# Last output projection tile, its norm and residual, and the first feed-forward tiles run by halves of the tokens

## What is computed

```python
    merged = jnp.sum(gates * projected, axis=2)
    x = x + rmsnorm(merged @ w_out[l], norm_mix_post[l])

    h = rmsnorm(x, norm_ffn_pre[l])
    f = (jax.nn.silu(h @ ffn_w_gate[l]) * (h @ ffn_w_up[l])) @ ffn_w_down[l]
    x = x + rmsnorm(f, norm_ffn_post[l])
```

## Time and profile before

| | |
|---|---|
| device time, median of 3 runs | 1585.75 us (1579.65, 1585.75, 1585.9) |
| span of the profiled execution | 1581.3 us |
| its own time | not given apart from its span |
| PE busy | 1508.4 us (95%), 7976 matmuls |
| DVE busy | 883.0 us (56%) |
| ACT busy | 596.3 us (38%) |
| mean DMA rate | 96 GB/s |

### The profile page before, as it was taken

One profiled execution on the slowest core, in us unless ns is written; L12 is line 12 of the kernel. 1 busy time (PEld: TensorE's weight loads), 2 busy tenths in 40 slices (PEclk: granted clock), 3 DMA queues, 4 the chain that ended last, 5 costly groups with the idle time before them and its releaser, 6 DMA issues.

```text
span 1581.3 us, 19613 instructions
## 1 busy us (share of the span) xinstructions
PE 1508.4 (95%) x7976; PEld 1205.2 (76%) x7976; DVE 883.0 (56%) x1405; ACT 596.3 (38%) x880; POOL 20.7 (1%) x36
## 2 busy tenths in 40 slices
PE   4799998999999999999999999999998999999997
PEld 2575786667787787777788887888886888888886
DVE  6889797785736763343525444643347544444234
ACT  3334415565325554232426433342333322222220
POOL 0010010000000000000000000000000000000000
PEclk8899999999999999999999999999999999999998
DMA  8433154104422111221223211232341323222221
GB/s 329 168 94 94 55 124 147 54 14 174 160 80 80 54 54 61 73 77 56 94 101 107 75 59 57 77 107 80 107 154 59 107 80 107 98 89 100 100 94 53
DMA packets 24472, 152.39 MB, mean 96 GB/s; under 512 B 3472, under 2 KB 6080, under 8 KB 8112
## 3 DMA queue, kind: packets, MB, share of 16 engines
q1 hardware_dynamic: 21872, 137.43, 24.3%
q0 software_dynamic: 2512, 13.72, 3.1%
HBM read 144.55 MB, written 7.88 MB: 96 GB/s over the span
## 4 chain that ended last, share of the span: by engine, by line
PE 86%; DVE 9%; ACT 2%; issue 1%; DMA 1%; SPq 0%; DVEq 0%; ACTq 0%
PE bank L552 85%; DVE score L2097 1%; PE bank L959 1%; DMA xr<-xT 1%; ACT w_hi L1208 1%; DVE score L2078 1%; DVE w_lo L1834 1%; DVE small L2077 1%; PE bank L891 0%; DVE sv L1791 0%; DVE rstd L1865 0%; DVE w_lo L1843 0%; DVE tval L2041 0%; DVE y_lo L1860 0%; DVE rstd L1906 0%
## 5 line engine op out<-in xcount | busy, mean ns | idle before, releaser
L552 PE MATMUL bank<-h_hi,w_hi 128*128 128x512 f32 (+1 forms) x1104 | 442.2, 401 | 13.5 <-DVE h_lo L2606 7.8
L552 PE MATMUL bank<-h_hi,w_lo 128*128 128x512 f32 (+1 forms) x1120 | 438.2, 391 | 0.0
L552 PE MATMUL bank<-h_lo,w_hi 128*128 128x512 f32 (+1 forms) x1104 | 432.0, 391 | 0.0
L1834 DVE TENSOR_TENSOR w_lo<-w_raw,w_hi 128x2048 fp32r<-128x2048 f32 (+2 forms) x106 | 239.2, 2257 | 245.1 <-ACT w_hi L1208 243.6
L1208 ACT CAST w_hi<-w_raw 128x2048 fp32r<-128x2048 f32 (+2 forms) x109 | 204.6, 1877 | 164.5 <-PE bank L552 161.6
L552 PEld LDWEIGHTS bank<-h_hi,w_hi 128*128 128x128 f32 (+1 forms) x1104 | 208.1, 188 | 73.5 <-issue 23.0
L552 PEld LDWEIGHTS bank<-h_hi,w_lo 128*128 128x128 f32 (+1 forms) x1120 | 210.9, 188 | 45.7 <-issue 0.4
L552 PEld LDWEIGHTS bank<-h_lo,w_hi 128*128 128x128 f32 (+1 forms) x1104 | 208.3, 189 | 42.9 <-issue 2.1
L552 PE MATMUL bank<-y_hi,w_hi 128*128 128x512 f32 x272 | 112.8, 415 | 4.6 <-DVE y_lo L1860 4.6
L552 PE MATMUL bank<-y_hi,w_lo 128*128 128x512 f32 x272 | 107.1, 394 | 0.0
L552 PE MATMUL bank<-y_lo,w_hi 128*128 128x512 f32 x272 | 106.9, 393 | 0.0
(11 more groups left out here) (374 smaller groups left out, 1871.2 us busy)
## 6 DMA issues: line engine op xcount, KB each, us to landing
w_raw<-wstream SPq DMA_DIRECT2D x120, 1024.0 KB, 4.8
xr<-xT SPq DMA_DIRECT2D x2, 2048.0 KB, 10.2
w_raw<-wstream SPq DMA_DIRECT2D x4, 768.0 KB, 4.2
bias_rows<-bias_table POOLq DMA_DIRECT2D x1, 2560.0 KB, 12.5
bias<-bias_rows POOLq DMA_DIRECT2D x1, 2048.0 KB, 12.4
x_saved<-xr POOLq DMA_DIRECT2D x1, 2048.0 KB, 9.6
xr<-x_saved POOLq DMA_DIRECT2D x1, 2048.0 KB, 8.1
outT<-down SPq DMA_DIRECT2D x16, 128.0 KB, 1.8
```

Of the source, the lines that this page charges most:

```text
L552: return pe.matmul(out, lhsT, rhs, start=start, stop=stop)
L1834: dve.tensor_tensor(w_low_of(s)[:, 0:kt, :], w_raw[:, i % RAW_SLOTS, 0:kt, :], hi_of(s)[:, 0:kt, :].bitcast(f32), ALU.subtract).then_inc(w ...
```

## The change

The fourth group of `out2` runs token half by token half: both feature halves for tokens 0 to 255 into two banks (semaphore `mid_done`), then for tokens 256 to 511 into two others. The post norm (statistic, root, reciprocal), the residual, `h_hi` and `h_lo` run for each half of the tokens. The statistic of half 0 is issued inside the matmuls of half 1, that of half 1 behind the first k step of `ffn_up`. PE runs `ffn_up[0]` and `ffn_up[1]` for token half 0 with four half groups at once, then for token half 1 with three, then the fourth. ACT copies the two banks of half 0 into `mo` before the next groups write there. The square for norm2 is still made for 512 tokens, in the second half. Slots of `w_hi` change parity behind `ffn_up[1]`, so that `ffn_up[2]` takes the slot of `out2[3]` and `ffn_up[3]` that of `ffn_up[0]`. DVE splits the weights of `ffn_up[2]` ahead of the seven additions for norm2 instead of behind them. `half_stats`, `half_root` and `half_rstd` replace the code of the last group too; there ACT now waits for both banks of a half before it squares the first.

```diff
-             ("y0", 8), ("y1", 8), ("merged", 8), ("norm2", 8), ("f", FT)]
+             ("y0", 8), ("y1", 8), ("merged", 8), ("norm2", 16), ("f", FT)]
...
-        sizes = {"norm0": 8, "q": 4, "k": 4, "norm1": 8, "norm2": 8, "post1": 8, "post2": 8}
+        sizes = {"norm0": 8, "q": 4, "k": 4, "norm1": 8, "norm2": 8, "post1": 10, "post2": 8}
...
-            ROOT[name] = i
+            ROOT[name] = i + (i > STATS.index("post1"))
...
-        LATE_BANKS = [3, 5, 6, LATE % GEMM_BANKS, 7, (LATE + 1) % GEMM_BANKS, (LATE + 2) % GEMM_BANKS]
+        MID_BANKS = [[(LATE + 1) % GEMM_BANKS, (LATE + 2) % GEMM_BANKS], [LATE % GEMM_BANKS, 7]]
+        LATE_BANKS = [3, 5, 6] + MID_BANKS[0] + MID_BANKS[1]
...
-            return w_wide[:, :, :] if s in WIDE else w_hi[:, s % 2]
+            return w_wide[:, :, :] if s in WIDE else w_hi[:, (s + (s > WIDE[0])) % 2]
+        def held_before(s):
+            return s - 3 if s in (WIDE[0] + 1, WIDE[0] + 2) else s - 2
...
-            for w, gr in enumerate(G["out2"]):
-                gemm(gr, "fm", h_hi, h_lo, need=AT["merged"],
-                     between=(lambda: presummed("post1")) if w == 3 else None)
-            last_stats("post1")
-            wide = [(gr, half, hi_of(gr.s), w_low_of(gr.s)) for gr, half in
-                    ((G["ffn_up"][0], 0), (G["ffn_up"][0], 1), (G["ffn_up"][1], 0))]
+            for gr in G["out2"][:3]:
+                gemm(gr, "fm", h_hi, h_lo, need=AT["merged"])
+            def half_stats(name, t):
+                c, s0 = end_cols(t), SQ0[name] + 6 + 2 * t
+                out = stat_bank(name)[:, c]
+                pe.wait_ge(root_ready, ROOT[name] + t)
+                pe.wait_ge(presum_ready, PRESUM.index(name) + 1)
+                mm(out, ones[:, :], rstd[:, c], True, False)
+                for half in range(2):
+                    pe.wait_ge(sq_ready, s0 + half + 1)
+                    mm(out, ones[:, :], sqb[:, half, c], False, half == 1).then_inc(sq_used, 1)
+            gr = G["out2"][3]
+            wh, wl = hi_of(gr.s), w_low_of(gr.s)
+            pe.wait_ge(w_low, gr.s + 1)
+            for half in range(2):
+                pe.wait_ge(bank_free[pbanks(gr)[half]], uses(gr, half))
+            pe.wait_ge(bank_free[MID_BANKS[1][0]], freed(G["out2"][2], 1))
+            for t in range(2):
+                for half in range(2):
+                    out, c = bank[MID_BANKS[t][half]][:, 0:HALF], slice(half * P, half * P + P)
+                    for k in range(KT):
+                        mm(out, wh[:, k, c], h_hi[:, k, end_cols(t)], k == 0, False)
+                        mm(out, wh[:, k, c], h_lo[:, k, end_cols(t)], False, False)
+                        ins = mm(out, wl[:, k, c], h_hi[:, k, end_cols(t)], False, k == KT - 1)
+                        if t == 1 and half == 0 and k == 3:
+                            half_stats("post1", 0)
+                    ins.then_inc(group_done if t else mid_done, 1)
+            wide = [(gr, half, hi_of(gr.s), w_low_of(gr.s)) for gr in G["ffn_up"][:2] for half in range(2)]
             pe.wait_ge(w_low, G["ffn_up"][1].s + 1)
             for gr, half, _, _ in wide:
                 if uses(gr, half):
                     pe.wait_ge(bank_free[pbanks(gr)[half]], uses(gr, half))
+            def wide_step(t, k, gr, half, wh, wl):
+                out, c = bank[pbanks(gr)[half]][:, end_cols(t)], slice(half * P, half * P + P)
+                mm(out, wh[:, k, c], h_hi[:, k, end_cols(t)], k == 0 and t == 0, False)
+                mm(out, wh[:, k, c], h_lo[:, k, end_cols(t)], False, False)
+                ins = mm(out, wl[:, k, c], h_hi[:, k, end_cols(t)], False, k == KT - 1 and t == 1)
+                if k == KT - 1 and t == 1:
+                    ins.then_inc(group_done, 1)
+            for t in range(2):
+                for k in range(KT):
+                    pe.wait_ge(act_low, AT["norm2"] + KT * t + k + 1)
+                    for step in wide[:4 - t]:
+                        wide_step(t, k, *step)
+                    if t == 0 and k == 0:
+                        half_stats("post1", 1)
             for k in range(KT):
-                pe.wait_ge(act_low, AT["norm2"] + k + 1)
-                for gr, half, wh, wl in wide:
-                    out, c = bank[pbanks(gr)[half]][:, :], slice(half * P, half * P + P)
-                    mm(out, wh[:, k, c], h_hi[:, k, :], k == 0, False)
-                    mm(out, wh[:, k, c], h_lo[:, k, :], False, False)
-                    ins = mm(out, wl[:, k, c], h_hi[:, k, :], False, k == KT - 1)
-                    if k == KT - 1:
-                        ins.then_inc(group_done, 1)
-            gemm_half(G["ffn_up"][1], 1, "fm", h_hi, h_lo)
+                wide_step(1, k, *wide[3])
...
-                    act.wait_ge(*tile_used(s - 2))
+                    act.wait_ge(*tile_used(held_before(s)))
...
-            root_of("post1", D)
+            def half_root(name, t, banks):
+                c, s0 = end_cols(t), SQ0[name] + 6 + 2 * t
+                for half in range(2):
+                    act.wait_ge(sq_used, s0 + half - 1)
+                    act.activation(sqb[:, half, c], banks[half], ACT.Square).then_inc(sq_ready, 1)
+                act.wait_ge(sq_used, s0 + 2)
+                act.wait_ge(rstd_ready, ROOT[name] + t)
+                act.activation(root[:, c], stat_bank(name)[:, c], ACT.Sqrt, bias=eps[:, 0:1],
+                               scale=1.0 / D).then_inc(root_ready, 1)
+            def wide_high(t, m):
+                c = end_cols(t)
+                act.wait_ge(x2_ready, KT * t + m + 1)
+                act.activation(h_hi[:, m, c], xr[:, m, c], ACT.Identity, scale=v("norm_ffn_pre", m)).then_inc(act_high, 1)
+                if t:
+                    act.activation(mo[:, m, :], xr[:, m, :], ACT.Square).then_inc(sq_ready, 1)
+            last = G["out2"][3]
+            act.wait_ge(mid_done, 2)
+            half_root("post1", 0, [bank[b][:, 0:HALF] for b in MID_BANKS[0]])
+            for half in range(2):
+                act.copy(mo[:, 6 + half, 0:HALF], bank[MID_BANKS[0][half]][:, 0:HALF])\
+                   .then_inc(bank_free[MID_BANKS[0][half]], 1)
             act.wait_ge(group_done, done("out2", 3))
+            wide_high(0, 0)
+            half_root("post1", 1, [bank[b][:, 0:HALF] for b in MID_BANKS[1]])
+            for m in range(1, KT):
+                wide_high(0, m)
+            ahead(G["ffn_up"][1])
             for m in range(KT):
-                act.wait_ge(x2_ready, m + 1)
-                act.activation(h_hi[:, m, :], xr[:, m, :], ACT.Identity, scale=v("norm_ffn_pre", m)).then_inc(act_high, 1)
-                act.activation(mo[:, m, :], xr[:, m, :], ACT.Square).then_inc(sq_ready, 1)
-            ahead(G["ffn_up"][1])
+                wide_high(1, m)
...
-                    act.wait_ge(end_done, 2 * t + half + 1)
...
+                act.wait_ge(end_done, 2 * t + 2)
+                half_root("post2", t, [bank[end_bank(t, half)][:, 0:HALF] for half in range(2)])
...
-            rstd_of("post1")
+            def half_rstd(name, t):
+                c = end_cols(t)
+                dve.wait_ge(root_ready, ROOT[name] + t + 1)
+                dve.reciprocal(rstd[:, c], root[:, c]).then_inc(rstd_ready, 1)
+                dve.wait_ge(rstd_ready, ROOT[name] + t + 1)
             last = G["out2"][3]
-            dve.wait_ge(group_done, 2 * last.g + 2)
             dve.wait_ge(x1_back, 16)
-            def wide_low(m):
-                dve.wait_ge(act_high, AT["norm2"] + m + 1)
-                dve.scalar_tensor_tensor(out=h_lo[:, m, :], in0=xr[:, m, :], scalar=v("norm_ffn_pre", m),
-                                         in1=h_hi[:, m, :].bitcast(f32), op0=ALU.mult, op1=ALU.subtract)\
+            def wide_low(t, m):
+                c = end_cols(t)
+                dve.wait_ge(act_high, AT["norm2"] + KT * t + m + 1)
+                dve.scalar_tensor_tensor(out=h_lo[:, m, c], in0=xr[:, m, c], scalar=v("norm_ffn_pre", m),
+                                         in1=h_hi[:, m, c].bitcast(f32), op0=ALU.mult, op1=ALU.subtract)\
                     .then_inc(act_low, 1)
-            for m in range(KT):
-                src = mo[:, m, :] if m < 6 else bank[pbanks(last)[m - 6]][:, :]
-                stt(sgb[:, m % 2, :], src, v("norm_mix_post", m), rstd[:, :], ALU.mult, ALU.mult)
-                if m >= 6:
-                    dve.nop().then_inc(bank_free[pbanks(last)[m - 6]], 1)
-                dve.tensor_tensor(xr[:, m, :], xr[:, m, :], sgb[:, m % 2, :], ALU.add).then_inc(x2_ready, 1)
-                dve.nop().then_inc(act_val, 1)
-                if m:
-                    dve.wait_ge(x2_ready, m)
-                    wide_low(m - 1)
-            dve.wait_ge(x2_ready, KT)
-            wide_low(7)
+            for t in range(2):
+                c = end_cols(t)
+                half_rstd("post1", t)
+                for m in range(KT):
+                    if m >= 6 and t == 0:
```

(45 more changed lines are left out.)

## The result

The changed kernel takes **1588.1 us** (median of 20 runs, 1581.5 to 1591.7), the kernel before 1584.8 (20 runs, 1579.7 to 1586.1): ratio 1.0020, 95% interval 1.0010 to 1.0029. That is 3 us slower, clear of noise, and less than the 0.5% that the prediction calls a change. Forecast were 1588.8 us and no change. The profiled execution took 1586.4 us with a span of 1584.4.

The account below looks back on a forecast made before the run. The prediction took PE (matmuls) to bound the kernel, with DVE's additions for norm2 the next late wait. Its terms 1.25 + 1.6 + 0.2 = 3.05 us, added to 1585.75, gave 1588.8 us; range 1582 to 1592.

Parts of the forecast that it names:

- The frame: Sum followed PE from the third output tile's end to ffn_up[2]'s first matmul; from there both kernels do the same work.
- Step 1: Fourth output tile in halves: PE loses 1.0 us waiting for a bank; DVE's reciprocal starts 4.3 us earlier.
- Step 2: Two hand-overs through ACT's h_hi, around the second half statistic: PE gaps of 1.4 and 1.8 us, DVE stopped until 1201.3.
- Step 3: DVE runs without pause from 1201.3; its norm2 additions end at 1228.15, PE waits 3.1 us, ffn_up[2] begins 1.25 us later.
- The slower rival: DVE's h_lo halves cost 0.66 us like whole tiles, adding 4.2 us on the path: 1593.0 us; chance 0.15.
- Step 4: Cold return: short gaps probably keep the clock, the 3.1 us gap before the norm2 statistic probably costs it: 1.6 us.
- The rival that rested on it: The clock also holds in the last gap, before the norm2 statistic: +1.45 us, 1587.2 us; chance 0.25.
- Step 5: Program end: ACT squares both banks of the last half only after the second is done: +0.2 us.
- Edits at nothing: Parts of the change counted as costing nothing, among them the ffn_up[3] split, with 4.5 us of cover.
- The head-start rival: ACT's halts at the hand-overs cost DVE nothing, DVE runs on from 1192.3: -3.4 us, 1582.4 us; chance 0.15.
- The absolute number: Whole-kernel forecast of 1588.8 us: the kernel before's median of 1585.75, 4.45 above its span, plus 3.05.

Follow-up runs that it names:

- e3: Changed kernel with PE's wait for the third tile's bank moved from ahead of token half 0 to ahead of half 1; 1588.1 us, one run.
- e5: Changed kernel with ACT's root of token half 1 behind the eighth h_hi tile, PE's second half statistic behind the fifth k step; 1585.5 us, ratio 1.0012.
- e6: Changed kernel with the first h_hi tile of token half 0 made before ACT waits for the whole fourth group; 1584.6 us, one run.
- e2: Changed kernel with DVE's weight split for ffn_up[2] put back behind the seven additions; 1586.7 us, ratio 1.0008.
- e4: Changed kernel with ACT's squares and root of half 1 behind the fourth h_hi, the second half statistic behind the fourth k step; 1586.5 us, ratio 1.0020.
- e1: Changed kernel with the norm2 statistic issued between the two halves of ffn_up[2] instead of ahead of it; 1587.2 us, ratio 1.0014.
- e7: e1 with ffn_up[3] cast and split ahead of the norm2 root and reciprocal, and ffn_up[4] one group earlier; 1583.8 us, ratio 0.9992.
- e8: Changed kernel with the edits of e1, e3, e5, e6 and e7, and the last group's squares one by one again; 1579.5 us, ratio 0.9969.
- e10: e8 with PE's second half statistic behind the fourth k step instead of the fifth; 1578.1 us, ratio 0.9959.
- e9: Kernel before, without the halving, with e7's edits (norm2 statistic between the halves of ffn_up[2], earlier weight splits); 1585.0 us, ratio 1.0003.

## Why the prediction was right, step by step

**The frame** held. The stage carries +2.8 us and the end +0.3, and there is no third place. Forecast were +3.05 on the span, measured +3.1; +3.3 between the medians.

**Step 1.** PE started at 1183.13 (forecast 1183.1) and the reciprocal half at 1192.48 (1192.3). e3 adds that this 0.9 us was wholly on the path. The prediction had carried it through its sum, but did not say so; asked for it alone I gave 0.5.

**Step 2.** `h_hi` half 0.51 us (taken: 0.50), PE again at 1197.45 and 1201.96 (1197.35, 1201.9), DVE standing until 1201.42 (1201.3). e5 and e6 confirm both hand-overs as path.

**Step 3** was the term with the wide bounds. `h_lo` halves start 0.40 us ahead of the next one, as taken; the additions ended at 1228.20 (1228.15) and PE's wait for them, from the moment at which its next matmul could have started, is 2.8 us (forecast 3.1; PE finished at 1225.5 and not 1225.0), 2.67 of them idle. That DVE's chain and not PE sets the end is shown by e5 and e2, by what a shorter chain gave; in e4 what a longer halt cost fits, once the clock is allowed for. The slower rival, small pieces at 0.66, fell with the 0.40.

**Step 4.** The clock fell behind the last gap and not behind the others, cost 1.49 us (1.6). But the forecast was a likely case, not a certain one, and its argument, that gaps of up to 1.8 us leave the clock whole and one of 3.1 does not, was weaker than it looked. The last section has a gap of 2.29 us, the same in both programs, that left the clock whole in the profile before and not in the one after, and two gaps of under 1 us that cost it. That it came out as forecast in the one profile that was compared is partly luck; without the cold return the span would have grown by 1.6 us. Of the five profiles with a last gap of 2.66 to 2.68 us four came back cold, and e4 did not:

```profile
1228.10:1230.80 2.70, 0.04 (x2) 0.02 (x1) 2.47 (x4) 0.00 (x0) 0.00 (x0) 1.00 0.90 316
1230.80:1234.20 3.40, 3.40 (x13) 2.51 (x14) 1.53 (x1) 2.25 (x2) 0.00 (x0) 1.00 0.44 186
```

So the rule that I weighed there, from the Trainium skill, "TensorE: Matmul & The Clock Gate", section "HAM oscillation — how this bites in real kernels", by which gaps this short do no harm, is contradicted by these traces four times out of five. The rival that rested on it is what e4 shows, and it is the rarer one.

**Step 5** was 0.2 and is 0.3.

**Edits at nothing** held in the changed kernel: its split of `ffn_up[3]` was ready at 1236.8, and wanted at 1231.36 + 45 x 0.227 = 1241.6. But e1 starts `ffn_up[2]` earlier and delays the norm2 factor, and the split behind it was the next thing late. The prediction had the size of the cover right (4.5 us; it was 4.8), and had the split behind the norm2 root. What it left open is that this order takes the cover away as soon as `ffn_up[2]` comes earlier and the statistic later.

**The head-start rival** (-3.4 us) fell, since DVE stood for ACT as forecast. It was too hopeful in its own terms too: with the 3.27 us halt taken away, e5 is 1.9 us of stretch below the changed kernel and still 0.9 above the kernel before, as the gap of 2.66 us ahead of the norm2 statistic stays, where the rival has no long gap. Below the kernel before came only the kernels in which the norm2 statistic and the splits had been moved too: e7 by 1.5, e8 by 5.6 and e10 by 6.7 us of stretch.

**The absolute number** was right partly by luck. It was built on a median of three, 1585.75, and a difference of 4.45 us between span and time. In the changed kernel's profiled run that difference is 2.0 us (1584.4 and 1586.4), and the median of 20 runs of the kernel before is 1584.8. The difference of 3 us was right (3.05 forecast, 3.3 measured), the base 1 us high.

## What to carry to other kernels

Cutting a stage in halves brings the first result early, but each engine's program now has twice the hand-overs, and one that stands in order ahead of work that could run (a root ahead of seven tiles that do not need it) hands the head start back. Then look for waits on a result that nobody needs yet: moving the one for the norm2 sum by half a group of matmuls, together with the weight splits that stood behind it, took 4.3 us off the stretch, 1.5 of them the cold return.

## What the runs showed of the hardware that I had not expected

A gap of 2.67 us of an otherwise full PE cost the clock in four profiles of five, with nearly the same program ahead of it: whether the clock falls is not fixed by the gap's length alone.

Places of the program that the change doesn't touch show it better. All twelve profiles have a gap of 2.3 us near 271 us, one of 2.08 near 321, and two of 0.93 and 0.97 us near 476, with 0.7 us of small matmuls between them. Behind the first, before and after:

```profile
272.80:277.00 4.20, 4.20 (x21) 3.43 (x22) 1.87 (x9) 2.86 (x6) 0.00 (x0) 1.00 0.44 187
```
```profile
272.10:275.50 3.40, 3.40 (x10) 2.63 (x9) 0.81 (x5) 2.45 (x5) 0.00 (x0) 0.50 0.02 7
```

Behind the second it is the other way round: the stretch at half clock is in the profile before, and after has 1.00 from 320.8 to 324.2. The pair of short gaps left the clock whole before (1.00 from 475 to 481 us) and cost it after:

```profile
476.90:480.30 3.40, 3.40 (x15) 2.60 (x12) 1.23 (x7) 2.21 (x10) 0.00 (x0) 0.50 0.35 149
```

Six of the twelve profiles (after, e1, e4, e5, e9, e10) are cold behind the first and behind the pair and warm behind the second, and the other six the reverse. So neither the length of one gap nor its being cut in two tells whether the clock falls. What does is not shown here. The gap of 7.82 us was followed by a cold return in both profiles that have it.

Whole runs differ ahead of the stage. The matmul at the start of the stretch began at 1118.7 us in one profile (e8) and at 1124.4 in another (e3), though all programs are the same up to there; all the profiles had cold stretches in the first 500 us, 37 to 61 us of them together, at different gaps. e3 had the most, but e8 had 44 us and not the least, so they do not explain the differences alone, and what else does stays open. Two edits of 1 us cannot be told apart by medians of a dozen runs here, and were by the stretch.
